# Six more expert tiles computed in two parts by tokens, and twelve parts behind the gates

## The reference, cut to what matters

```
q = x @ w_query                      # 8 heads, two halves of 128
s = q . sub_keys                     # 128 keys on each half; top 16 of each, then top 16 of the pairs
gate = softmax(top 16 scores)        # expert index = 128 * i1 + i2
a = gelu(u_tab[expert] . x)
out = sum over heads and picks of gate * a * v_tab[expert]
```

## Time and profile before

| | |
|---|---|
| median of 3 runs | 3063.93 us (3054.43 to 3065.33) |
| the profiled execution | 3061.89 us |
| its span, first to last instruction | 3060.1 us |
| mean granted TensorE clock | 0.965 |
| PE / PEld busy | 92% / 80% |
| DVE / ACT / POOL busy | 78% / 28% / 43% |
| DMA | 796 MB, 260 GB/s over the span |

### The profile page before, as it was taken

The page is one execution under the profiler, slowest core; times in us unless marked ns, Lnnn a source line. Parts: engine busy times, 40 slices in busy tenths (PEclk is TensorE's granted clock), DMA queues, the critical chain, the costliest instruction groups (busy, mean ns, idle before and its releaser), DMA issues. The chain is left out here.

```text
span 3060.1 us, 42913 instructions
## 1 busy us (share of the span) xinstructions
PE 2819.4 (92%) x15144; PEld 2446.3 (80%) x15144; DVE 2401.9 (78%) x5125; ACT 849.3 (28%) x1272; POOL 1330.3 (43%) x1088
## 2 busy tenths in 40 slices
PE   7999999798999999999989998899969988899897
PEld 5777777586998999999989997888758767677776
DVE  5676556533768989989679996899769888899998
ACT  4223333222322222222222221255322222222223
POOL 0000000001214666566446664077747677765551
PEclk8999999899999999999999999999989999999999
DMA  4111111123338999999779997279999999999995
GB/s 173 43 43 43 57 44 55 64 83 131 126 105 300 346 357 383 366 354 395 286 283 354 362 363 274 73 207 268 318 364 400 400 399 392 381 398 407 407 407 194
DMA packets 359877, 795.99 MB, mean 260 GB/s; under 512 B 34408, under 2 KB 165996, under 8 KB 357536
## 3 DMA queue, kind: packets, MB, share of 16 engines
q0 software_dynamic: 124832, 424.38, 36.4%
q1 hardware_dynamic: 168048, 331.75, 29.8%
q10 hardware_dynamic: 66832, 37.78, 4.3%
HBM read 695.62 MB, written 98.18 MB: 259 GB/s over the span
## 5 line engine op out<-in xcount | busy, mean ns | idle before, releaser
L1286 PE MATMUL u_p<-hn_hi,u_hi 128*128 128x384 f32 (+2 forms) x1856 | 630.6, 340 | 63.1 <-DVE u_lo L1280 41.6
L1287 PE MATMUL u_p<-hn_lo_r,u_hi 128*128 128x384 f32 (+2 forms) x1856 | 623.5, 336 | 0.0
L1288 PE MATMUL u_p<-hn_hi,u_lo 128*128 128x384 f32 (+2 forms) x1856 | 623.4, 336 | 0.0
L1791 POOL DMA_INDIRECT s_ring<-in_peer_u,row_idx x264 | 341.3, 1293 | 277.6 <-DVE s_dots L1922 151.0
L1286 PEld LDWEIGHTS u_p<-hn_hi,u_hi 128*128 128x128 f32 x1856 | 355.5, 192 | 76.1 <-DVE u_lo L1280 47.4
L2249 PE MATMUL y_p<-v_hi,w_hi 128*128 128x512 f32 x1024 | 327.4, 402 | 89.1 <-DVE w_lo L2334 89.1
L2204 POOL DMA_INDIRECT y_ring<-in_peer_v,late_cols x256 | 308.7, 1206 | 169.1 <-DVE y_late L2347 101.4
L2347 DVE SCALAR_TENSOR_TENSOR y_late<-y_ring,late_cols,y_late 128x1024 f32<-128x1024 f32 x256 | 329.1, 1286 | 48.3 <-DMA y_ring<-in_peer_v,late_cols 28.3
L1287 PEld LDWEIGHTS u_p<-hn_lo_r,u_hi 128*128 128x128 f32 x1856 | 355.5, 192 | 2.3
L1288 PEld LDWEIGHTS u_p<-hn_hi,u_lo 128*128 128x128 f32 x1856 | 355.2, 191 | 2.5
L1922 DVE CUSTOM_DVE_ANT_0 s_ring<-s_ring,yt 128x1024 f32<-128x1024 f32 x260 | 318.0, 1223 | 31.8 <-DVE s_dots L1922 2.2
(11 more groups left out here) (409 smaller groups left out, 5194.9 us busy)
## 6 DMA issues: line engine op xcount, KB each, us to landing
u_raw<-in_peer_ut SPq DMA_DIRECT2D x106, 512.0 KB, 6.9
act_scratch<-act_tile SPq DMA_DIRECT2D x128, 256.0 KB
late<-in_peer_v SPq DMA_DIRECT2D x32, 1024.0 KB, 9.3
down_raw<-in_peer_v SPq DMA_DIRECT2D x32, 1024.0 KB
hn_lo<-in_peer_ut SPq DMA_DIRECT2D x48, 512.0 KB
wp_raw<-in_w_heads SPq DMA_DIRECT2D x64, 256.0 KB, 3.4
late<-in_w_query SPq DMA_DIRECT2D x16, 1024.0 KB, 6.1
late_act_scratch<-act_tile SPq DMA_DIRECT2D x128, 128.0 KB, 6.3
```

The lines of the kernel that those rows point to most:

```text
L1286: mm(b, uh[:, r % 3, k, :], hn_hi[:, k, t], start=(k == 0), stop=False)
L1287: mm(b, uh[:, r % 3, k, :], hn_lo[:, k, t], start=False, stop=False)
L1288: last = mm(b, ul[:, r % 3, k, :], hn_hi[:, k, t], start=False, stop=(k == ND - 1))
L1791: nc.gpsimd.indirect_dma_start(out=ring[:, s, :], out_offset=None, in_=src, in_offset=bass.IndirectOffsetOnAxis(ap=idx[:, column:column + ...
```

## The change

Six more tiles are computed in two parts (`NLATE` 30 to 36). K2 still has 108 visits: twelve sections of seven as before, three sections of eight (LATER and FULL in turn), and a last section with none, where it was fifteen of seven and a last one of three. The loop over the gates keeps its 24 EARLY parts, so behind it there are 12 instead of 6. 20 rows instead of 24 are added there, which leaves 68 instead of 64 to the down stage's first 15 pairs. SP issues `tile_in` of four parts instead of two ahead of its wait for the gate stores.

```diff
-NLATE = 30
-E_K1, E_D1, E_K2, E_D2 = 10, 4, 78 + NLATE, 6
+NLATE = 36
+E_K1, E_D1, E_K2, E_D2 = 10, 4, 72 + NLATE, 6
...
-TAIL = 24
+TAIL = 20
...
-KINDS = ([FULL] * (E_K1 + E_D1) + [FULL, LATER, FULL, FULL, LATER, FULL, FULL] * (NLATE // 2) + [FULL] * (3 + E_D2)
+KINDS = ([FULL] * (E_K1 + E_D1) + [FULL, LATER, FULL, FULL, LATER, FULL, FULL] * 12 + [LATER, FULL] * 12 + [FULL] * E_D2
          + [EARLY] * NLATE)
...
-            FIRST_U = [E0 + 7 * min(s, NLATE // 2) + 3 * max(s - NLATE // 2, 0) for s in range(NSEC + 1)]
+            FIRST_U = [E0 + 7 * min(s, 12) + 8 * min(max(s - 12, 0), 3) for s in range(NSEC + 1)]
...
-            for e in range(R0, R0 + 2):
+            for e in range(R0, R0 + 4):
                 tile_in(sp, e)
             for s in range(2):
                 sp.wait_ge(saved[s], 16 * NJ + 16)
             for s in range(2):
                 Pair(sem, s, late[:, s * SLOT:(s + 1) * SLOT]).load(sp, A, a_dram, g_dram, s)
-            for e in range(R0 + 2, NJOB):
+            for e in range(R0 + 4, NJOB):
                 tile_in(sp, e)
```

## The result

The changed kernel takes 3110.04 us (median of 4 runs, 3101.64 to 3117.50), the kernel before beside it 3064.63 (4 runs, 3054.43 to 3070.05): ratio 1.0137, 95% interval 1.0113 to 1.0161. It is slower, and by more than the range allowed: 3082 was forecast, with 3066 to 3094 around it. The profiled execution took 3104.94 us, with a span of 3102.8 and a mean granted clock of 0.959.

The account below looks back on a forecast made before the run. No engine bounds the whole: DVE in K2's later sections, a DMA behind the gates, the DMA limit in the down stage. From 3061.9: -12 + 0 + 26 + 5 = +19, so 3081, said as 3082; range 3066 to 3094.

Parts of the forecast that it names:

- K2: Sections 12 to D2: three more u_lows start section 15 3.4 us later, sample products end earlier; gain 12 us (2 to 17).
- The last section: Section 15 in K2: PE, idle 17 us, starts sample products at 1880.4, partly at half clock, and ends at 1897.8.
- near enough: Sample products in K2: by the skill's cold-start rule K2 would gain 2 us (all matmuls at half clock 27.7), sum 3092.
- K2 gives nothing: Rival in K2: the sample products stay at half the clock, gain 2 us, total 3092; chance 0.10.
- Behind the gates: Stage after the gates: ninth part's load queues behind the gate-store wait and pair loads, PE idle 22 us; +26 us.
- Twelve parts without a wait: Rival behind the gates: gate store lands by 2212.7, within 27 us, so the ninth part is in time; 3057; chance 0.14.
- The down stage: Last stage: four more rows, 2.1 MB, with the DMA engines full; +5 us, bounds 0 and 6.
- The four rows are hidden: Rival in the down stage: PE is the fuller engine and prefetch hides the rows; total 3076; chance 0.14.

Follow-up runs that it names:

- e9: Changed kernel with the eight-visit sections in the order FULL, LATER instead of LATER, FULL: 3092.09 us, ratio 1.0056.
- e2: Changed kernel with fifteen sections of seven visits again and a last one of three LATER parts: 3100.17 us, ratio 1.0083.
- e1: Changed kernel with eight tile_ins instead of four ahead of SP's wait for the gate stores: 3084.68 us, ratio 1.0054.
- e12: e6 with ten visits' loads and stores instead of eight ahead of the wait: 3069.44 us, ratio 0.9995.
- e4: Changed kernel with 8 rows instead of 20 behind the gates (TAIL 8): 3109.80 us, ratio 1.0136.
- e3: Changed kernel with 24 rows instead of 20 behind the gates (TAIL 24): 3105.23 us, ratio 1.0113.
- e10: e6 with 24 rows instead of 20 behind the gates (TAIL 24): 3068.92 us, ratio 0.9993.
- e7: Kernel before with the last section's u_lows in its first two gaps instead of six: 3060.03 us, ratio 0.9973.
- e6: Changed kernel with e2's sections, the last section's u_lows in its first two gaps, and e1's eight tile_ins ahead of the wait: 3067.70 us, ratio 0.9996.

## Why the prediction was wrong

**K2 is the step that failed**, in the sentence "So section 15 starts 3.4 us later, at 1863.3". It priced an eighth visit as one more `u_low` of DVE, since DVE was the bound, and put waits of DVE for ACT at nothing without a reason. Measured, the three sections grew by 17.5 us: 3.4 for the `u_low`s, as priced, and 14.1 of such waits. The cause is a ring of waits. The rounding `u_high` of visit e needs PE to have finished visit e - 3; the `u_low` of visit e needs the rounding; PE needs the `u_low`. In a section of LATER and FULL in turn, the third visit is a part, a third of a FULL tile's work (2.8 of 8.42 us), and the `u_low` of the fourth stands 23.7 us behind the section's start in either order (1705.75 in the changed kernel, 1709.17 in e9). PE is through with the short part long before and waits 6.81 us (1707.01). The sixth visit, a FULL tile behind the next queries, is late by that. The rounding for the next section's first visit needs it, and comes at 1739.83, and DVE waits 5.66 us for it in its last gap. With FULL first, PE has 8.4 us of work in the place of 2.8: in section 12 of e9 it waits for no `u_low` longer than 1 us, and DVE waits for ACT in none of the three sections. The order alone doesn't do it: in e2, with seven visits and the same short third one, PE waits as long (6.82 us in section 12), but no section grows, since there the next section's first rounding needs the fifth visit and not the sixth. It takes both, the eighth visit and the short one first. e9's gain against the kernel before is 13.3 us, where 12 was forecast. So the gain forecast in K2 was there to be had with eight visits, and the order of two kinds of visit took it away.

**The last section** came as forecast. The sample products start 17.2 us after its first instruction (17.1 forecast: 1880.4 less 1863.3) and take 15.9 us (17.4 forecast, 13.9 at the full clock), and DVE adds them 33.2 us after it (34.5 forecast). PE had been idle for 13.8 us (17 forecast). The granted clock was 0.50 up to 1905, 0.84 from there to 1910, then 1.00. The rule of the Trainium skill that was weighed there (TensorE: Matmul & The Clock Gate, "HAM oscillation") is for pieces of work shorter than the waits between them. Here PE had no wait over 0.1 us between the rows once the first had landed, so this trace doesn't test the rule; what was wrong is the "near enough" by which the prediction applied it, and with it the 27.7 us. The rival that leaves the products at half the clock, K2 gives nothing, had the right size (+0.8 us) for the wrong reason.

**Behind the gates** was right in the terms that ended last: the store landed 49.4 us after its issue (49.0 forecast), 16.7 us from SP's passing the wait to the end of the ninth part's `u_low` (17.1), 26.7 us from there to the next stage (26.7), 26.3 us in all (26). On the way there it was less exact. The last gather was to be asked for at about 2218, on the scale of before; it was issued at 2235.8, 2228 on that scale, since DVE's additions stand behind the `u_low` of the seventh part, whose load was late. PE was done with the eighth part at 2239.3, 2 us later than forecast, and idle for 20.2 us (22 forecast). That the ninth load queues behind the wait and the pair loads is shown by e1 and e12, which take it out of the queue and get 16.5 and 22.6 us back. The rival Twelve parts without a wait needed the store to land within 27 us, and even with 8 gathers it took 34.8. That rival took equal shares of the time, about half for the store; its share was 27.2% before and 27.8% after, and what changed the landing was how much was asked for in all. The Trainium skill (DMA: Bandwidth & Descriptors, "Queues, rings and completion order") has the engines take turns packet by packet and says nothing of equal times; no run here tests the turns themselves.

**The down stage** was mis-sized: +8.8 us, 5 forecast and 6 the upper bound. Up to the 25th pair the four rows cost what was worked out: it is 290.6 to 292.9 us from the first pair in the five kernels with 24 rows behind the gates, 295.4 to 297.4 in the eight with 20, and 315.3 in e4. But the whole stage doesn't follow the four rows. From the first pair to the last the kernels with six parts behind the gates take 773.5 to 777.0 us, those with twelve 782.1 to 786.1, with 20 rows or 24 (785.7 and 783.2 in e3 and e10). Those two lose their lead of 5 us from the 25th pair to the 37th (165.6 and 166.1 us, where the eight with 20 rows take 158.0 to 164.1, the kernel before 155.9 and e7 160.5), in waits of DVE for gathered rows. So the 5 us of the forecast is not shown as a cost of the stage, and its rival, The four rows are hidden, is neither shown nor refuted: with twelve parts, 24 rows instead of 20 gave no shorter stage (+3.4 us in e3, -2.1 in e10). What the +8.8 goes with in these runs is the twelve parts; why stays open, and no run here takes that stretch apart.

**Chance between executions.** Some 8 us of the difference between the two profiles lie ahead of section 12. From 400 to 600 us the granted clock was 0.96 in the profile of before and 0.93 in that of after, but in e9 it was 0.97 and K2 started late all the same (959.1), so where the time goes stays open. The sum was made against one profile that was earlier than most: later sets of the kernel before have medians of 3068 to 3070. The changed kernel's median, of four runs, is itself some 9 or 10 us above what the stages of e1 and e6 make of it. With the 35 us of the stages alone the time would be 3097, which is over the range of 3066 to 3094 too.

In numbers: of the 35 us (18 or 19 forecast) by which the stages behind section 12 grew, K2 is 12.8 over the forecast, the down stage 3.8 over, and the rest within 1.5.

## What to carry to other kernels

Where several engines pass buffers in a ring, an engine that looks full isn't proof that one more piece costs only its own duration: walk the ring for each order of long and short pieces, and ask whether the short one leaves the next engine with nothing to do until an operand placed at a fixed point of another engine's program. Behind a hand-written wait on a queue, count what is issued after it, and take it in front if it doesn't need what is waited for; but a stage ended sooner may give nothing if the first transfers of the next were what it would wait for anyway. And compare an expected gain of a few us with the spread between two profiles, stage by stage, before it is put into a sum.

## What was unexpected of the hardware

A store of 4 MB in packets of 511 bytes, alone on its queue, landed the later the more was asked for meanwhile on other queues: 20.4 us in the median of the eight, and the last of them 34.8 us with 8 gathers of 512 KB issued behind it, 49.4 with 20, 53.4 with 24, 57.9 with 20 and four more tile loads and activation stores, and 62.2 with 24 and those four (e10). Its share of the DMA engines was 27.2% beside 24 gathers and 27.8% beside 20 with two more tile loads and activation stores. A tile load of 512 KB that went out beside it in the changed kernel, at 2212.07, took 17.7 us, where 6.9 is the median of such loads in the kernel before.
